# Prompt attention: the order of transposes and score matmuls on TensorE

## The reference

```python
s_s = jnp.einsum('bqgrd,bgqkd->bgrqk', q, k_s) * scale + bias_s      # selected blocks
p_s = masked_softmax(s_s, (dist_s >= 0)[:, :, None])
o_s = jnp.einsum('bgrqk,bgqkd->bqgrd', p_s, v_s)
...
s_w = jnp.einsum('bqgrd,bkgd->bgrqk', q, kw) * scale + bias_w        # a window of 512
p_w = masked_softmax(s_w, mask_w)
o_w = jnp.einsum('bgrqk,bkgd->bqgrd', p_w, vw)
return gates[..., 0:1] * o_c + gates[..., 1:2] * o_s + gates[..., 2:3] * o_w
```

## Time and profile before

| | us |
|---|---|
| runs shown | 1428.22, 1429.99, 1431.51 |
| median | 1429.99 |
| profiled execution, its own time | 1433.1 |
| its span, first to last instruction | 1431.0 |
| TensorE busy in the span | 1241.3 |
| VectorE busy | 723.6 |
| ScalarE busy | 542.5 |

### The profile page before, as it was taken

One profiled execution on the slowest core, in us unless ns is written; L12 is line 12 of the kernel. 1 busy time (PEld: TensorE's weight loads), 2 busy tenths in 40 slices (PEclk: granted clock), 3 DMA queues, 4 the chain that ended last, 5 costly groups with the idle time before them and its releaser, 6 DMA issues. The chain is left out here.

```text
span 1431.0 us, 21333 instructions
## 1 busy us (share of the span) xinstructions
PE 1241.3 (87%) x7878; PEld 903.9 (63%) x7879; DVE 723.6 (51%) x1452; ACT 542.5 (38%) x910; POOL 111.2 (8%) x167
## 2 busy tenths in 40 slices
PE   3299999999957999999998997289999999999862
PEld 1156666666546656666666885267788887788730
DVE  0012221222233455666666765788658568685148
ACT  0000000000022667656554221276546466564132
POOL 1000001100000000000000000001001011010050
PEclk9599999999956899999999998599999999999986
DMA  9843334400054522000004332699769669894582
GB/s 321 270 150 135 129 128 136 72 23 13 10 166 151 204 77 43 1 1 2 1 2 157 118 118 81 237 373 361 270 236 354 250 240 376 302 319 163 200 301 95
DMA packets 89697, 235.57 MB, mean 165 GB/s; under 512 B 7450, under 2 KB 15061, under 8 KB 89463
## 3 DMA queue, kind: packets, MB, share of 16 engines
q1 hardware_dynamic: 76711, 192.19, 39.0%
q0 software_dynamic: 8144, 27.62, 5.3%
q10 hardware_dynamic: 4768, 14.75, 2.7%
HBM read 196.49 MB, written 40.13 MB: 165 GB/s over the span
## 5 line engine op out<-in xcount | busy, mean ns | idle before, releaser
L2188 PE MATMUL psum<-w_hi,x_parts 128*128 128x512 f32 x736 | 239.0, 396 | 10.6 <-DVE x_parts L2307 9.8
L2300 DVE TENSOR_TENSOR w_lo<-raw,w_hi 128x2048 fp32r<-128x2048 f32 x96 | 215.6, 2287 | 58.1 <-ACT w_hi L2247 58.0
L2247 ACT CAST w_hi<-raw 128x2048 fp32r<-128x2048 f32 x96 | 178.6, 1914 | 83.1 <-DVE work L2318 51.2
L595 PE MATMUL psum<-low,high 128*128 128x512 f32 (+5 forms) x576 | 200.6, 502 | 0.0
L2188 PEld LDWEIGHTS psum<-w_hi,x_parts 128*128 128x128 f32 x736 | 138.9, 189 | 42.3 <-issue 13.6
L595 PEld LDWEIGHTS psum<-low,high 128*128 128x128 f32 (+1 forms) x576 | 105.4, 188 | 77.9 <-issue 67.2
L2188 PE MATMUL psum<-w_lo,x_parts 128*128 128x512 f32 x368 | 143.9, 391 | 0.0
L1496 DVE CUSTOM_DVE_ANT_0 low<-psum,high 128x512 f32<-128x512 f32 (+5 forms) x172 | 93.2, 579 | 78.1 <-PE psum L1197 67.0
L2188 PE MATMUL psum<-w_hi,a_parts 128*128 x368 | 120.5, 399 | 5.9 <-DVE a_parts L2313 5.9
L1409 ACT ACTIVATE low<-low,high 128x640 f32<-128x640 f32 (+9 forms) x140 | 98.8, 708 | 44.5 <-DVE high L1496 44.1
L1227 PE MATMUL psum<-keep,low 128*128 128x128 f32 (+1 forms) x556 | 103.5, 293 | 11.5 <-ACT high L1420 4.8
(11 more groups left out here) (317 smaller groups left out, 1437.9 us busy)
## 6 DMA issues: line engine op xcount, KB each, us to landing
raw<-in_moe_w_gate SPq DMA_DIRECT2D x16, 2048.0 KB, 11.2
raw<-in_moe_w_up SPq DMA_DIRECT2D x16, 2048.0 KB
raw<-in_moe_w_down SPq DMA_DIRECT2D x16, 2048.0 KB, 11.4
high<-in_w_mod SPq DMA_DIRECT2D x12, 2048.0 KB, 13.9
y_d<-work ACTq DMA_DIRECT2D x24, 512.0 KB, 7.0
high<-in_x_prompt SPq DMA_DIRECT2D x16, 512.0 KB, 3.9
y_d<-high SPq DMA_DIRECT2D x1, 8192.0 KB, 23.6
low<-in_w_in SPq DMA_DIRECT2D x3, 2048.0 KB, 15.6
```

The lines of the kernel that those rows point to most:

```text
L595: mm = pe.matmul(c.bank(2 + n % 2)[0:T, 0:w], hT[i % 2][:, k, 0:T], c.w_in[:, k, a:a + w], start=(k == 0), stop=(k == KT - 1))
L2188: mm = pe.matmul(out, left[l][:, k * P:(k + 1) * P], w[:, bass.ds(at + k * step, 512)], start=n == 0, stop=n == len(steps) - 1)
L2247: act.copy(c.w_hi[:, at:at + PART // 2], c.raw[:, o:o + PART // 2]).then_inc(hi_done[p], 1)
L2300: dve.tensor_tensor(c.w_lo[:, at:at + PART // 2], c.raw[:, o:o + PART // 2], c.w_hi[:, at:at + PART // 2].bitcast(F32), ALU.subtract).then ...
```

## The change

On TensorE, step n turned group 0's first four blocks, then did the first piece of the scores, then turned group 0's rest and group 1's first four, then did the second piece, then turned group 1's rest. Now it turns group 0 whole, does all pieces of the scores, then turns group 1 whole. Where pair n - 2 has one turn for each group (`n_turn` = 1), both groups are turned ahead of the scores. On VectorE, the copy of group 0's rest comes ahead of both pieces' softmax instead of between them.

```diff
                 if n_turn:
                     turn(n - 2, 0, 0)
-                if n_piece:
-                    scores(n, 0)
+                if n_turn == 1:
+                    turn(n - 2, 1, 0)
                 if n_turn == 2:
                     turn(n - 2, 0, 1)
-                if n_turn:
+                for m in range(n_piece):
+                    scores(n, m)
+                if n_turn == 2:
                     turn(n - 2, 1, 0)
-                if n_piece == 2:
-                    scores(n, 1)
-                if n_turn == 2:
                     turn(n - 2, 1, 1)
```

```diff
                 two = 0 <= n - 2 < N and blocks(n - 2) > 4
-                if n_piece:
-                    soft(n, 0)
                 if two:
                     turned(n - 2, 0)
-                if n_piece == 2:
-                    soft(n, 1)
+                for m in range(n_piece):
+                    soft(n, m)
                 if two:
                     turned(n - 2, 1)
```

## The result

| kernel | median us | lowest to highest | runs |
|---|---|---|---|
| before | 1431.95 | 1428.22 to 1437.36 | 13 |
| changed | 1437.41 | 1432.20 to 1447.84 | 13 |

The ratio of changed to before is 1.0042, 95% interval 1.0021 to 1.0062: the change makes the kernel slower, by about 6 us (3 to 9). The profiled execution took 1432.2 us, its span is 1430.1 us. That is the lowest time of the 13 and less than the profiled execution of before. The two spans alone would mislead: the stage begins at 437.25 us here and at 441.89 in before, and nothing ahead of it was changed. So I compare stretches inside the stage, counted from its own start.

A forecast was written before the change was run, and what follows sets the result against it. TensorE's instruction stream was taken to set the stage's time. Gains of 24.8 us against costs of 26.2, with exponentials starting 0.4 earlier at the end, gave +1.0 us in all: 1431 us, range 1421 to 1440.

The forecast's parts named there:

- Gain 1: Steps with two pieces: one run of turns and one of scores fewer, fixed costs of 0.36 each, 11.5 us saved.
- Gain 2: Two-turn steps: group 1's turns no longer wait for ScalarE's copy of group 0's first turn, 9.6 us saved.
- Costs 1 and 2: Two-turn steps: group 0's rest waits behind a scale turn, 4.7 us; small results wait behind group 1's first turn, 7.1 us.
- Gain 3: One-turn steps: one run of turns fewer in 36 steps, 3.7 us saved.
- costs 3 to 6: Mostly one-turn steps: new waits behind scale turns, sample values and compressed work, and at the stage's start, 14.4 us lost.
- Cost 3: Seven one-turn steps behind a scale turn: group 1's turn waits for the scale copy, 5.8 us lost.
- cost 4: Six steps behind a sample's values: group 1's turn waits for VectorE to free its bank, 3.8 us lost.
- the 8 us more: Scores followed directly by values: extra saving if no fixed cost stood between them; the sum assumed the cost stays.
- Rival (b), the clock: One-turn steps: new waits bring two more falls to half clock, 6 to 7 us longer, 1438; chance 0.20.
- (a): One-turn steps: waits are not additive, so their 14.4 us of new costs halve, 1424; chance 0.25.
- (d): Waits for group 0's copy come back because exponentials and copies end later, +6 us, 1437; chance 0.07.
- (c): Fixed costs stay because the array's drain is paid per piece of scores, 1442; chance 0.08.

The follow-up runs named there:

- one_not_scale: New order only in one-turn steps of the kernel before, except the seven behind a scale turn, which keep the old order; 1436.28 us in one run.
- two_only: Kernel before with the new order only in two-turn steps, and VectorE's new order; 1422.38 us, ratio 0.9956 to before.

## Why the prediction was right, and where it was off

The forecast was 1431 us, within 0.2% of before, range 1421 to 1440; measured are 1437.41 and +0.42%. The time lies inside the range and the sign that had the largest chance, slower (0.37), is the one that came. But the sum itself said +1 us and not +6, so the time was met by the width of the range and not by the sum. Of the 6.4 us between 1431 and 1437.41, 2.0 are the base: I had added to a median of 1429.99 from three runs, and 13 give 1431.95. The other 4.5 are what the change costs beyond the +1 of the sum.

- **What bounds.** Right. TensorE's stream sets the stage, and each of its new waits lengthened it.
- **Gain 1** (11.5 us). Right as a mechanism: the pieces back to back take 1.28, predicted 1.27. The fixed cost of a run of scores is paid once for both pieces.
- **Gain 2** (9.6 us). Right: in the two-turn stretch the waits for the copy L1420 of before are gone but for two at the stage's end, which weren't in the 9.6. But my reading of the list was wrong: I took the 24 weight loads that wait for the exponentials and the waits for L1420 as one thing, and said that the 24 would go. They are 22 in the changed kernel. In the two-turn stretch they were 12 (5.0 us), and only five of these, 0.58 us and longer, stood at a late turn of group 1, the last of them at the stage's end; the others are 0.17 to 0.32. Eight (2.2 us) are left, seven of 0.17 and the one at the end. The 9.6 came from the spacings, and doesn't rest on this row.
- **Costs 1 and 2** (4.7 and 7.1 us). Right in place and count. From the spacings: the eight waits behind the scale turn come to 5.1 us (1.22 - 0.42 = 0.80 in the fence above, 0.46 predicted for that step), the eleven of small results to 7.6 (0.83 with one block, 0.78 predicted; my own prices make 7.3 for the eleven, where I wrote 7.1). That piece 0 covered the scale turn's bank in before was not quite so either: group 0's rest waited for L1449 there in two cases, 0.4 us. So the two-turn stretch gained 7.5 where 21.1 - 11.8 = 9.3 were forecast; 0.9 of the 1.8 are these two, the rest is open.
- **Gain 3 and costs 3 to 6** (3.7 against 14.4 us). Right in sign and place: 10.7 net forecast, 11.0 and 12.0 in the traces of equal low clock. Cost 3, less its share of gain 3, is 5.9 against 5.8. That the sum is so near is in part luck, since the terms are less exact one by one. By the spacings the seven waits for the scale copy come to 7.0 us, and before had 0.7 of them already. The six waits behind a sample's values come to 6.1 where cost 4 had 3.8. On the other side, the sample keys' second half waited 0.96 and 0.68 in before and 0.47 once in the changed kernel, which I had not counted. Further, the bias waits have grown from 1.75 to 2.47 each, as forecast, and the gates' is 0.87; the idle times ahead of the turns behind a sample's values are 0.41 to 1.49 each. Scores of 512 columns followed directly by values take 1.07, where 1.06 was the price ahead of turns:

```profile
570.42 1.13 PE L1197 MATMUL psum<-high 64*128 64x512 f32 x4
571.49 1.09 PE L1242 MATMUL psum<-high 128*64 128x128 f32 x16
```

  So the fixed cost stays there, as I had taken it, and the 8 us more did not come. The trace agrees here with the Trainium skill, TensorEngine Tiling (Array Packing), Key Properties, by which a change of tiling mode drains TensorE.
- **The moved copy at nothing.** Right for the change as made, by the stretch; but it is a part that earns 1.7 us, and I had not said so.
- **Rival (b), the clock.** I gave further falls 0.20, as an alternative, and a spread belongs to them in the sum. I also read the one-piece steps of before as having one fall, where the same trace has a first one of 30.7 us at the start of the stage. In three traces each, the low clock grew from 35.2 to 44.4 us in the mean, and the stretch by 14.8 where 11 to 12 are the order's at equal low clock; so 3 to 4 us of time lie in the clock. "More stretches at 1.2 GHz" was one of my signs of being wrong, and it came in two of three traces. Whether the change causes it or the three traces of before had fewer falls by chance stays open. That transposes would count less as work for the clock, as the Trainium skill, TensorE: Matmul & The Clock Gate, Part 4, has it, no run here shows; the trace of the changed kernel speaks against it as far as it goes: in its two-turn steps, some with runs of eight transposes on either side of the scores, the granted clock stayed at 1.00. Rivals (a), waits that are not additive, and (d), waits that come back, did not come: one_not_scale gives back the whole price of cost 3, and two_only has the two-turn stretch 7.5 us shorter. (c) is refuted by the 1.28.

## What to carry to other kernels

Between two uses of a PSUM bank that alternates, whatever stands on TensorE is the cover for the copy out of it: ahead of moving work together, list for each instruction who held its bank two uses before and behind what that reader queues. A new order can be right for one shape of step and wrong for another; here it is worth -7.5 us where steps have two pieces of scores and +11 to +12 where they have one. Made conditional, as in two_only, it gives the gain without the loss. Spacings of starts show waits that idle times hide, and a stretch counted from its own start shows a few microseconds that whole times of +-5 us don't.

## What the runs showed of the hardware

The start of the stage lies anywhere between 436.6 and 443.5 us in 14 traces whose code ahead of it is the same, and the granted clock falls at different places in the same kernel: within 514 to 516 us in one trace of before, within 478 to 480 in another, and in a third it has not yet risen at 476 us. The two-turn stretch, where no clock falls, repeats to 0.1 us. In the one-turn stretch of the changed kernel 10.2 us more of low clock came with 3.8 and 4.1 us more time; before differs by 1.0 us between two traces with the same low clock, so not all of the spread is the clock's.
